# A two-layer transformer step with experts: router sums taken beside w_out, token-major rows scaled last, one block per layer

## What is computed

```
for l in range(2):
    h = rms_norm(x) * (1 + scale1) + shift1
    z = h @ w_in[l]                         # fourier | gqa q,k,v | diff q,k,v | 3 gates
    merged = sum_b sigmoid(gate_b) * (branch_b @ w_b[l])
    x += gate1 * (merged @ w_out[l])
    t = rms_norm(x, norm2_g[l]) * (1 + scale2) + shift2
    scores = sigmoid(t @ w_router)          # 16 experts in 4 groups
    # best group by scores + bias, top 2 experts in it, weights w / sum(w)
    x += gate2 * sum_e combine_e * (silu(t @ w_gate_e) * (t @ w_up_e)) @ w_down_e
y = rms_norm(x)
```

## Time and profile before

| | us |
|---|---|
| runs before, median of 3 | 2298.21 (2296.72 to 2300.35) |
| profiled execution | 2301.7 |
| its span, first to last instruction | 2299.9 |
| TensorE busy | 2032.7, 88% of the span |
| DVE, ACT, POOL busy | 1028.2, 854.0, 351.2 |
| mean granted TensorE clock | 0.943 |

### The profile page before, as it was taken

One profiled execution on the slowest core, in us unless ns is written; L12 is line 12 of the kernel. 1 busy time (PEld: TensorE's weight loads), 2 busy tenths in 40 slices (PEclk: granted clock), 3 DMA queues, 4 the chain that ended last, 5 costly groups with the idle time before them and its releaser, 6 DMA issues. The chain is left out here.

```text
span 2299.9 us, 30545 instructions
## 1 busy us (share of the span) xinstructions
PE 2032.7 (88%) x12439; PEld 1644.5 (72%) x12439; DVE 1028.2 (45%) x1692; ACT 854.0 (37%) x1347; POOL 351.2 (15%) x133
## 2 busy tenths in 40 slices
PE   6999879999999964999949998878999997399994
PEld 4789756678888943667637897657888895267663
DVE  3266246721111145777661662674111113477773
ACT  3333335431111232556433333654111113256553
POOL 2313100012222202000033132000222220200003
PEclk9999889999999987999969998999999998699997
DMA  8211586841212027898542112001212112599964
GB/s 292 77 37 57 182 293 223 258 137 55 83 55 74 19 95 289 309 310 306 203 163 73 38 57 66 1 1 37 83 56 83 56 37 96 195 404 403 310 214 174
DMA packets 163854, 339.30 MB, mean 148 GB/s; under 512 B 10370, under 2 KB 121346, under 8 KB 149252
## 3 DMA queue, kind: packets, MB, share of 16 engines
q1 hardware_dynamic: 151488, 302.65, 37.9%
q0 software_dynamic: 5760, 20.97, 2.4%
q10 hardware_dynamic: 6468, 13.73, 1.6%
HBM read 337.58 MB, written 53.74 MB: 170 GB/s over the span
## 5 line engine op out<-in xcount | busy, mean ns | idle before, releaser
L615 POOL TENSOR_TENSOR wlo<-raw,whi 128x2048 fp32r<-128x2048 f32 x52 | 238.3, 4586 | 1175.2 <-ACT whi L640 1175.2
L1559 DVE TENSOR_TENSOR xw_gu_lo<-xw_gu_raw,xw_gu_hi 128x2048 fp32r<-128x2048 f32 x100 | 228.3, 2285 | 27.9 <-ACT xw_gu_hi L1350 27.8
L184 PE MATMUL psum<-h_hi,whi 128*128 128x320 f32 x896 | 216.9, 323 | 22.4 <-POOL h_lo L177 19.6
L184 PE MATMUL psum<-whi,h_hi 128*128 128x256 f32 x720 | 210.0, 292 | 0.0
L184 PE MATMUL psum<-h_lo,whi 128*128 128x320 f32 x896 | 205.4, 310 | 0.0
L184 PE MATMUL psum<-h_hi,wlo 128*128 128x320 f32 x896 | 205.2, 310 | 0.0
L184 PE MATMUL psum<-whi,h_lo 128*128 128x256 f32 x720 | 203.5, 283 | 0.0
L184 PE MATMUL psum<-wlo,h_hi 128*128 128x256 f32 x720 | 203.4, 282 | 0.0
L1350 ACT ACTIVATE xw_gu_hi<-xw_gu_raw 128x2048 fp32r<-128x2048 f32 x100 | 185.5, 1907 | 0.0
L784 ACT ACTIVATE sig_m<-psum 128x640 f32<-128x640 f32 x48 | 33.8, 705 | 400.5 <-PE psum L184 400.4
L1700 PE MATMUL psum<-xw_d_raw,act_T 128*128 128x512 f32 x400 | 180.0, 592 | 0.9 <-ACT act_T L1376 0.9
(11 more groups left out here) (250 smaller groups left out, 3569.1 us busy)
## 6 DMA issues: line engine op xcount, KB each, us to landing
xw_gu_raw<-w_e_gate SPq DMA_DIRECT2D x50, 1024.0 KB
xw_gu_raw<-w_e_up SPq DMA_DIRECT2D x50, 1024.0 KB
xw_d_raw<-w_e_down SPq DMA_DIRECT2D x50, 1024.0 KB, 8.3
raw<-w_in SPq DMA_DIRECT2D x46, 1024.0 KB, 5.3
wm_rest<-w_mod SPq DMA_DIRECT2D x40, 1024.0 KB, 5.2
h_sel<-h_rows SPq DMA_DIRECT2D x50, 512.0 KB, 6.3
y_rows<-y_sel SPq DMA_DIRECT2D x50, 512.0 KB, 9.5
h_rows<-c_zero ACTq DMA_DIRECT2D x1, 12800.0 KB, 52.9
```

The costliest lines, as they stand in the source:

```text
L184: mm = pe.matmul(dst, st, mv[q], start=start and n == 0, stop=stop and n == 2)
L615: pool.tensor_tensor(wlo[i % 2][:, :, :], raw[i % 2][:, :, :], whi[i % 2][:, :, :].bitcast(F32), ALU.subtract).then_inc(w_lo, 1)
L1559: dve.tensor_tensor(gu_lo[i % 2][:, n, :, :], gu_raw[i % 2][:, n, :, :], gu_hi[i % 2][:, n, :, :].bitcast(F32), ALU.subtract).then_inc(x_l ...
```

## The change

**The w_out loop.** With `g = norm2_g * (1 + scale2)` (`mul2`), `t @ W` equals `rstd * ((x * g) @ W) + shift2 @ W`, since `rstd` is one number per token. ACT now makes `xm = x_T * mul2` in the loop, DVE makes the squares, and TensorE takes four narrow products per feature block (`route_sums`): the router product of `xm` and the sum of squares, each for tokens 0 to 383 and 384 to 639, written to four 32-partition strips of PSUM bank 6. Beside them `shift2` is laid out as rows (`shift_row`, by four products of ones with diagonal matrices that ACT made) and its router product is taken (`swr`, `crow`).

**After the loop.** The sums are copied, turned by three transposes, and only then rooted and inverted, token-major (128x5). The logits are scaled there. The token-major rows are made tile by tile (`turn_tok`): a one-row product of the tokens' standard deviations with `shift_row`, then eight transposes of `xm` over it in PSUM, and ACT scales the whole by `rs2` when it copies. Three tiles stand ahead of the rank products, two behind them. The features of a row stand in another order, which the expert loads already have.

**Blocks.** The `clear()` between mixing and experts is gone: two blocks per program are left. SP issues the expert loads behind waits on the last weights and products of the loop, POOL waits for each tile's copy, and ACT in layer 1 issues its five small loads behind the scaling. The rank products become one group of six (before: five and five).

```diff
+                    act.wait_ge(g_pfull, 24)
+                    for s in range(2):
+                        for kc in range(KD):
+                            ins = act.activation(diag[:, s, kc, :], ident[:, :], ACT.Copy, scale=shift2[:, kc, s:s + 1])
...
                     for f in range(KD):
                         act.wait_ge(o_add, f + 1)
-                        square(act, n2, sq2, f)
+                        act.activation(xm[:, f, 0:P], x_T[:, f, 0:P], ACT.Copy, scale=mul2[:, f, 0:1])
+                        act.activation(xm[:, f, P:TOK], x_T[:, f, P:TOK], ACT.Copy, scale=mul2[:, f, 1:2]).then_inc(r_x, 1)
...
-                    root(act, n2, var2)
+                    act.activation(junk[:, 0:1], eps[:, :], ACT.Sqrt)
...
+                        dve.tensor_tensor(sq2[:, f % 2, :], x_T[:, f, :], x_T[:, f, :], ALU.mult).then_inc(r_q, 1)
...
-                    rstd_of(dve, n2, var2, rstd2)
...
+                    def route_sums(f):
+                        pe.wait_ge(r_x, f + 1)
+                        pe.wait_ge(r_q, f + 1)
+                        for q in range(4):
+                            c0, w = ((0, 3 * P), (3 * P, 2 * P))[q // 2]
+                            st = ones[:, 0:32] if q % 2 else wr[:, f * NE:f * NE + 32]
+                            mv = sq2[:, f % 2, c0:c0 + w] if q % 2 else xm[:, f, c0:c0 + w]
+                            mm = pe.matmul(psum[32 * q:32 * q + 32, 6, 0:w], st, mv, start=(f == 0), stop=(f == KD - 1))
+                        mm.then_inc(r_lg, 1)
...
-                            sum_squares(pe, n2, sq2, f - 1)
-                    sum_squares(pe, n2, sq2, KD - 1)
-            clear()
-
-
-            with nc.Block() as block:
+                            route_sums(f - 1)
+                        if 1 <= f <= 4:
...
+                            pe.matmul(psum[:, 7, :], ones[:, :], diag[:, s, 4 * hf:4 * hf + 4, :].rearrange("p k c -> p (k c)"),
...
+                    route_sums(KD - 1)
...
+                    sp.wait_ge(w_lo, N_STREAM - ahead)
                     load_gate_up(0)
+                    sp.wait_ge(o_full, KD)
                     load_gate_up(1)
...
                     for t in range(TT):
+                        pool.wait_ge(k_a, t + 1)
...
+                    for q, w in ((1, 3 * P), (3, 2 * P)):
+                        ins = act.activation(std_row[32 * q:32 * q + 1, 0:w], sums[32 * q:32 * q + 1, 0:w], ACT.Sqrt,
+                                             bias=eps[32 * q:32 * q + 1, :], scale=1.0 / D)
+                    ins.then_inc(r_sd, 1)
...
+                    for t in range(TT):
+                        act.wait_ge(k_t, t + 1)
+                        act.activation(h_tok[:, t, :].rearrange("p (l m) -> p l m", l=KD),
+                                       flat(tile_pair[t])[:, :].rearrange("p (m l) -> p l m", l=KD), ACT.Copy,
+                                       scale=rs2[:, t:t + 1]).then_inc(k_a, 1)
...
+                    dve.wait_ge(r_lg, KD)
+                    dve.tensor_copy(sums[:, 0:2 * P], psum[:, 6, 0:2 * P])
+                    dve.tensor_copy(sums[0:64, 2 * P:3 * P], psum[0:64, 6, 2 * P:3 * P]).then_inc(r_lk, 1)
...
+                    def turn_tok(t):
...
+                        for hf in range(2):
+                            pe.matmul(dst[:, hf, :], std_row[rows, c0:c0 + P], shift_row[rows, int(t > 0), hf * 512:(hf + 1) * 512],
+                                      start=True, stop=False)
+                            for kc in range(4):
+                                mm = pe.matmul(dst[:, hf, kc * P:(kc + 1) * P], xm[:, 4 * hf + kc, t * P:(t + 1) * P], ident[:, :],
+                                               is_transpose=True, start=False, stop=(kc == 3))
                         mm.then_inc(k_t, 1)
```

More of the change, by code:

```diff
@@ L133, in build @@
         n1 = [sem(f"norm1_{x}") for x in ("squares", "summed", "var", "std", "rstd")]
-        n2 = [sem(f"norm2_{x}") for x in ("squares", "summed", "var", "std", "rstd")]
         def square(act, st, sq, kc):
@@ L670, in _ @@
                         modulate_act(act, h_mix, mul1, shift1, kc)
+                    if not first:
+                        small_loads()
                     act.wait_ge(m_l, 2)
@@ L1530, in _ @@
                                                   op0=ALU.mult, op1=ALU.add))
-                    step(dve.tensor_tensor(slot[:, :], slot[:, :], top2[:, :], ALU.mult))
+                    step(dve.tensor_tensor(slot[:, :], slot[:, :], top2[:, 0:TT * NE], ALU.mult))
                     step(dve.tensor_reduce(pos_f[:, 0:TT], e3(slot), AX.X, ALU.max))
@@ L1657, in _ @@
+                    pe.wait_ge(r_sd, 1)
+                    for t in range(3):
+                        turn_tok(t)
                     pe.wait_ge(r_c, 32)
                     pe.wait_ge(r_st, ROUTE_STEPS + 1)
-                    pe.matmul(psum[:, 0, 0:TT * NE], before[:, :], top2[:, :], start=True, stop=False)
-                    for m in range(1, TT):
-                        pe.matmul(psum[:, 0, m * NE:TT * NE], ones[:, :], top2[:, 0:(TT - m) * NE], start=False, stop=(m == TT - 1))
-                    for t in range(TT):
-                        mm = pe.matmul(psum[:, 1, 0:NE], ones[:, :], top2[:, t * NE:(t + 1) * NE], start=(t == 0), stop=(t == TT - 1))
+                    pe.matmul(psum[:, 5, 0:(TT + 1) * NE], before[:, :], top2[:, :], start=True, stop=False)
@@ L1664, in _ @@
+                    for m in range(1, TT + 1):
+                        mm = pe.matmul(psum[:, 5, m * NE:(TT + 1) * NE], ones[:, :], top2[:, 0:(TT + 1 - m) * NE],
+                                       start=False, stop=(m == TT))
                     mm.then_inc(r_rk, 1)
+                    for t in range(3, TT):
+                        turn_tok(t)
                     def turn_h(i):
```

183 lines of the change are left out of this document (106 added, 77 removed).

## The result

| | before | changed |
|---|---|---|
| runs beside each other, median of 4 each | 2299.28 (2296.72 to 2303.96) | 2263.00 (2258.12 to 2266.21) |
| ratio, 95% interval | | 0.9838 (0.9811 to 0.9865) |
| profiled execution, its span | 2301.7, 2299.9 | 2260.26, 2258.5 |
| mean granted clock | 0.943 | 0.947 |

The change saves 36 us. The forecast was 2246.0 us with a range up to 2261; the measured median is 17 us above the forecast and 2 us above the range. The sign was right and most of the mechanism. One step was wrong, the clock that term C gave to the token tiles, and term A was half of its true size.

The account below looks back on a forecast made before the run. It took the chain from last w_out product to first expert product as the bound; layer 1 -25.5, layer 0 -24.7, with E -52.2 us, from the median 2298.2 to 2246.0 us, range 2239 to 2261.

Parts of the forecast that it names:

- term C: Token tiles ahead of the rank products: first at 1.2 GHz, next two at 2.4 GHz, +2.5 us a layer (0 to 7.7).
- term A: The w_out loop gets longer through narrow products at 0.8 us a round and four shift products: +1.5 us (0.3 to 10.5).
- B: Last w_out product to the scores shrinks to 7.1 us: -25.7 us in layer 0, -26.5 us in layer 1.
- D: Rank products, six left with the clock kept up, take 1.6 us: -3.0 us a layer (-1.8 with the clock low).
- first row write to experts: Stretch from the row writes to the first expert product: nothing changes, 27.9 us stay.
- E: Start of layer 1: ACT's first scaling no longer waits behind five small loads, -2.0 us once (0 to -2.1).
- What bounds the kernel: In each layer, one chain from the last w_out product to the first expert product, 77.0 us in layer 1.
- the rival of serial groups: Column groups in the w_out loop don't overlap: 10.5 us more per layer, 2267 us; chance 0.08.
- the rival on the other side: Slower than before: narrow products let the clock fall inside the w_out loop, up to 2364 us; chance 0.02.
- the clock stays low: One-row products are too little work for TensorE's clock through the tiles: 6.4 us more per layer, 2259 us; chance 0.18.
- The premise that the gap costs the clock: TensorE, mostly idle for 4 us ahead of the tiles, falls to 1.2 GHz there.
- Hidden, with 5 us to spare: Last two tiles and ACT's copies, at worst 12.4 us, fit before the ninth row write, 17.8 us behind the rank result.

Follow-up runs that it names:

- r1_changed: The changed kernel, unaltered, in a second round of runs: 2267.27 us, ratio to before 0.9851.
- e2: Changed kernel with three more 512-column products of ones, results unread, filling the idle gap ahead of the tiles: 2255.98 us, ratio 0.9805.
- e11: Kernel with 128-row tile products, each made as four products of 32 tokens in four column groups: 2248.7 us, a single run.
- e3: Changed kernel with the tiles' one-row products made 128 rows deep through a zero-padded operand: 2249.61 us, ratio 0.978.
- e9: Kernel with 128-row tile products and low parts behind the row writes, plus two shift-diagonal products moved from the w_out loop into the gap: 2238.33 us, ratio 0.9736.
- e4: Changed kernel with the tiles' one-row products left out, so a tile is eight transposes and lacks the shift: 2248.17 us, ratio 0.9772.
- e5: Kernel with 128-row tile products, with VectorE's low parts of the first expert's weights waiting until the row writes have landed: 2247.08 us, ratio 0.9764.
- e1: Changed kernel with two token tiles instead of three ahead of the rank products: 2257.09 us, ratio 0.9807.

## Why the prediction was right and wrong

Per layer, in the profiled executions, layer 1 unless two values stand (layer 0 / layer 1):

| step | forecast | measured |
|---|---|---|
| A, w_out loop | +1.5 | +3.1 / +3.1 |
| B, last product to scores | -25.7 / -26.5 | -25.7 / -26.5 |
| C, tiles ahead of the rank products | +2.5 | +9.0 / +9.2 (`r1_changed` +10.3) |
| D, rank products | -3.0 | -1.85 |
| rank result to first row write | 0 | -0.6 / -0.5 |
| first row write to experts | 0 | -1.7 / -1.9 |
| E, once | -2.0 | -2.0 |

The measured ones add up to -38.2 us; the spans differ by 41.4. Of the remaining 3.2 us, 0.9 lie ahead of layer 0's w_out loop and 2.2 between its first expert product and layer 1's w_out loop; no edit was tried on them.

The median flatters the forecast. Terms A, C and D together are 18.7 us worse than forecast in the two layers; the 4.7 us of the row writes and these 3.2 us came unforeseen and on the other side. Without them the changed kernel would be near 2271 us.

- **What bounds the kernel** was read rightly: the chain from the last w_out product to the first expert product was the place, and what left it left the time.
- **A** had the mechanism and missed the size. The column groups overlap: the eight records of a round start within 0.35 us, so the rival of serial groups is out. But a round costs 8.01 - 6.96 = 1.05 us, not 0.8. The size was scaled from a row in which two rounds of 256 columns follow one another; here each round stands alone between products of the whole array, so it goes to another tiling and back by itself. The 0.3 us that `e2` and `e11` show for such a pair of changes is about the 0.25 us that were missing; no run isolates it. With four shift products of 0.86 us it is 6 x (1.05 - 1.15) + 3.6 = +3.0, and the loops are 3.1 us longer (58.74 against 55.65 us from the first to the last addition). The loop kept its clock of 1.00, and the rival on the other side didn't come.
- **B** was right to 0.1 us, hand-overs included.
- **C is the step that failed.** It took one tile at the lower clock and let the others have the full one, because transposes alone had brought the clock back in the earlier trace rows and half of a tile is transposes. With one-row products between them it did not come back: 6.1 us a tile, all five. That clock is the large part of the miss. A smaller one is the price of a tile: the term's bound with all three tiles at the lower clock was 7.7 us, and in `r1_changed`, where they all were, it is 10.3, because half a tile is 3.05 us at 1.2 GHz where the rows had given 2.6. The rival "the clock stays low" stood in the prediction with 2259 us and 0.18; the experiments show that it was this rival, by the mechanism that it named (a one-row product is too little work), and that the argument held against it was about another kind of instruction.
- **The premise that the gap costs the clock** holds only in part. In the changed kernel the first half tile still ran at 1.00 in its profile; in others (`r1_changed`, layer 1; `e3`, layer 0) the clock fell in the gap. What decides is what the tiles do afterwards.
- **D** followed C: at 0.50 the rank products cost what the low-clock end of the term said, -1.8. At the full clock, in `e3`, their result is read 1.55 us behind their start, where the forecast had 1.6.
- **"Hidden, with 5 us to spare"** for the last two tiles holds only just: with 6.1 us a tile the last copy ends 38 us behind the addition and the ninth write, the first that needs it, is issued at 40.
- **Row writes**: the forecast left 27.9 us unchanged. They became 26.0 because the late tiles hold up ACT, therefore `hi(0)`, therefore DVE's `lo(0)`, which no longer stands beside the row writes. In the trace of before, DVE's `lo(0)` began at 1973.96 and the third and fourth write of layer 1 took 2.43 and 1.89 us; I had not asked why. Nothing in the forecast stood for this gain, so it is luck. So is the 0.5 to 0.6 us ahead of it, where POOL's first write starts 0.3 us behind the end of DVE's `rows_ab` instead of 0.8; why is not shown.
- **E** was right: the trace gives 2.0, undoing it costs 2.2.

Without the low clock the same program lies at 2249.6 (`e3`), 3.6 us above the forecast, of which A's surplus in two layers would explain 3.0. By the median and by where its clock falls, the forecast fits a kernel with full-depth tiles.

## What to carry to other kernels

Price TensorE's clock by the form of the work that runs at it, not by whether the engine is busy: here the clock stayed at 1.2 GHz through 26 us of unbroken work with one-row products in it, and it stayed low with 32 and 64 rows as well, while padding one operand with zero rows gave 13 to 18 us in two layers for one memset each (`e3`). When an operation is moved into an idle gap, look for work of the kernel itself that fits there (`e9`: two products moved, 3.5 us less in the loops of the two layers and 3.7 us less behind them). And when a transfer's issue time varies between equal instructions, ask which engine runs beside the slow ones before taking the sum as fixed; and look at the DMA share before counting on a sooner issue for a sooner landing.

## What was not expected of the hardware

- TensorE lost the full clock while 100% busy (`e2`: 1.00, 0.86, 0.50 in three stretches without idle), with products of 1 row between transposes; the same with 32 and 64 rows. Why the depth matters was not settled, nor what lies between 64 and 128 rows, nor whether a change of tiling by rows has a part in it.
- 24 transposes alone brought it back (`e4`, layer 0).
- What a half tile costs more with a one-row product than with a 128-row one: 0.34 us at the full clock, 0.49 at the lower one (3.05 against 2.56, the latter 827.70 to 830.26 in `e3`). The change of tiling is the likely reason: with four column groups and full depth it is 0.28 us more.
- GpSimd's row writes take 1.9 to 3.0 us to issue instead of 0.95 while VectorE subtracts two SBUF operands.
- A row write behind nine others lands 4.87 us after its start with nothing on VectorE (`e5`, DMA share 0.98 to 0.99), and 3.49 us after it where GpSimd had paused (`e1`). A faster issue is in part given back there.
